# Two transformer blocks on one core: rope operands of 128 rows, evictions ahead of a panel's last split, the latents' inverse root moved from the transposes to the eviction

## What is computed

```python
# first block
h = rms_norm(x, norm_g)
qa, ka, va, ga, qb, kb, vb, gb = split(h @ w_in)                  # 2048 x 8192
ya = stick_breaking_attention(qa, ka, va)                         # 8 heads of 128
yb = chunk_band_attention(qb, kb, vb, q_gain, k_gain, rel_bias)   # 8 heads of 128
x = x + concat(ya * silu(ga), yb * silu(gb)) @ w_out
# second block; c gives six rows: mod = silu(c) @ w_ada + b_ada
sh1, sc1, gt1, sh2, sc2, gt2 = split(mod, 6)
z = (rms_norm(x, g_pre_mix) * (1 + sc1) + sh1) @ w_in_2
cq, ckv, kr, qs, ks, vs, gates = split(z)                         # 768, 512, 64, 2048, ...
q = rms_norm(cq, g_q_lat) @ w_uq        # MLA: 16 heads of 128 + 64 (rope)
kv = rms_norm(ckv, g_kv_lat) @ w_ukv
s = (q_nope @ k_nope.T + rope(q_rope) @ rope(kr).T) * 192 ** -0.5 # causal softmax, @ v
mix = (sigmoid(g_a) * o_mla + sigmoid(g_b) * o_window) @ w_o
x = x + gt1 * rms_norm(mix, g_post_mix)
u = causal_conv3((rms_norm(x, g_pre_ffn) * (1 + sc2) + sh2) @ w_up)
x = x + gt2 * rms_norm((silu(u_gate) * u_up) @ w_down, g_post_ffn)
```

## Time and profile before

| | |
|---|---|
| median of 3 runs | 1977.7 us (1974.12 to 1988.61) |
| profiled execution | 1984.85 us |
| its span | 1982.5 us |
| TensorE busy | 1933.0 us, 98% |
| VectorE busy | 1360.7 us, 69% |
| ScalarE busy | 1049.2 us, 53% |
| GpSimd busy | 119.0 us, 6% |
| mean granted clock of TensorE | 0.997 of 2.4 GHz |

### The profile page before, as it was taken

How to read it: one execution, slowest core, us unless ns; L and a number is a source line. 1 busy time by engine, 2 the same in 40 slices (tenths; PEclk the granted TensorE clock), 3 DMA queues, 4 the chain that set the end, 5 groups by cost and what they waited for, 6 DMA issues and landing times.

```text
span 1982.5 us, 30450 instructions
## 1 busy us (share of the span) xinstructions
PE 1933.0 (98%) x9804; PEld 1612.4 (81%) x9804; DVE 1360.7 (69%) x1838; ACT 1049.2 (53%) x1687; POOL 119.0 (6%) x197
## 2 busy tenths in 40 slices
PE   6999999999999999999999999999999999999998
PEld 5888887778888777778888778888888888888886
DVE  5677776667787745558877767777777776655555
ACT  5544545554455554446764444565656655544444
POOL 1000001101000003331110000000000000000000
PEclk9999999999999999999999999999999999999999
DMA  7788776578888853357678875677777765555554
GB/s 255 273 285 266 242 257 222 183 252 291 282 278 288 301 165 115 115 156 216 201 239 282 305 259 168 214 232 231 236 229 228 238 206 185 174 186 190 192 194 143
DMA packets 233657, 444.82 MB, mean 224 GB/s; under 512 B 14189, under 2 KB 105930, under 8 KB 232186
## 3 DMA queue, kind: packets, MB, share of 16 engines
q1 hardware_dynamic: 230890, 430.20, 65.6%
q0 software_dynamic: 2704, 13.82, 2.2%
HBM read 439.72 MB, written 4.24 MB: 224 GB/s over the span
## 4 chain that ended last, share of the span: by engine, by line
PE 86%; DVE 5%; ACT 3%; issue 3%; DMA 2%; SPq 0%; POOL 0%; DVEq 0%; ACTq 0%; POOLq 0%
PE PS L1659 53%; PE PS L1978 17%; PE PS L1979 8%; PE PS L1753 2%; ACT w_hi L621 1%; DVE arena L1075 1%; PE PS L1764 1%; PE PS L1695 1%; PE PS L1756 1%; PE PS L1739 1%; DVE w_lo L1025 1%; DMA ada_raw<-in_w_ada 1%; PE PS L1774 1%; PE PS L1775 1%; PE PS L1772 1%
## 5 line engine op out<-in xcount | busy, mean ns | idle before, releaser
L1025 DVE TENSOR_TENSOR w_lo<-raw,w_hi 128x1024 fp32r<-128x1024 f32 x618 | 755.3, 1224 | 499.4 <-ACT w_hi L621 491.6
L1659 PE MATMUL PS<-w_hi,aT 128*128 128x512 f32 (+1 forms) x3264 | 1046.1, 394 | 10.7 <-DVE arena L1059 2.4
L621 ACT ACTIVATE w_hi<-raw 128x1024 fp32r<-128x1024 f32 x618 | 653.8, 1060 | 643.3 <-PE PS L1659 431.1
L1659 PEld LDWEIGHTS PS<-w_hi,aT 128*128 128x128 f32 x3264 | 612.2, 188 | 152.2 <-issue 10.2
L1659 PE MATMUL PS<-w_lo,aT 128*128 128x512 f32 (+1 forms) x1632 | 633.6, 388 | 0.0
L1978 PE MATMUL PS<-aT,w_hi 128*128 128x512 f32 x1408 | 499.4, 400 | 2.1 <-DVE aT L1154 2.1
L1979 PE MATMUL PS<-aT,w_lo 128*128 128x256 f32 x1408 | 395.9, 281 | 0.0
L1659 PEld LDWEIGHTS PS<-w_lo,aT 128*128 128x128 f32 x1632 | 307.2, 188 | 58.3 <-issue 0.2
L1978 PEld LDWEIGHTS PS<-aT,w_hi 128*128 128x128 f32 x1408 | 265.0, 188 | 68.2 <-DVE aT L1154 2.3
L1979 PEld LDWEIGHTS PS<-aT,w_lo 128*128 128x128 f32 x1408 | 266.5, 189 | 0.2 <-issue 0.2
L1075 DVE SCALAR_TENSOR_TENSOR arena<-ada_raw,silu_c,arena 128x1024 f32<-128x1024 f32 x192 | 247.6, 1289 | 10.6 <-DMA ada_raw<-in_w_ada 10.4
(11 more groups left out here) (215 smaller groups left out, 1298.8 us busy)
## 6 DMA issues: line engine op xcount, KB each, us to landing
raw<-in_w_in SPq DMA_DIRECT2D x256, 512.0 KB, 3.9
ada_raw<-in_w_ada SPq DMA_DIRECT2D x192, 512.0 KB, 4.8
raw<-in_w_up SPq DMA_DIRECT2D x176, 512.0 KB, 3.5
raw<-in_w_down SPq DMA_DIRECT2D x88, 512.0 KB, 3.8
raw<-in_w_out SPq DMA_DIRECT2D x32, 512.0 KB, 5.4
raw<-in_w_o SPq DMA_DIRECT2D x32, 512.0 KB, 5.4
raw<-in_w_uq SPq DMA_DIRECT2D x18, 512.0 KB, 4.9
raw<-in_w_ukv SPq DMA_DIRECT2D x16, 512.0 KB, 4.0
```

The lines of the kernel that those rows point to most:

```text
L621: nc.scalar.activation(w_hi[:, m % RING, :], raw[:, m % RING, :], ACT.Copy).then_inc(hi_ready, 1)
L1025: nc.vector.tensor_tensor(w_lo[:, m % RING, :], raw[:, m % RING, :], w_hi[:, m % RING, :].bitcast(F32), ALU.subtract).then_inc(lo_ready, 1)
L1659: mm = pe.matmul(dst, l, r, start=first and j == 0, stop=last and j == 2)
```

## The change

1. `krT` and `qrT` get 128 rows instead of 64; GpSimd sets rows 64 to 127 to zero once, after the key's rope part is transposed. ScalarE still writes 64 rows.
2. VectorE and ScalarE evict a panel ahead of their split of slot 7 instead of behind it: `copy_out` in the QKV panels, `add_out` in the projection with w_out, `o_out` and `mix_squares` in that with w_o, and ScalarE's evictions of the latent panels (the 320-column one too).
3. In the stick-breaking panels the head pieces (with `sb_P`) stand between the split and the ada piece, not behind both. In the band panels `stage_b` stands at the start of its slot.
4. The latents are transposed without a diagonal. Their inverse root is the scale of ScalarE's evictions of Q and KV; a semaphore `lat_inv` says that it is there. The squares of the 768 columns of cq go to SBUF instead of PSUM, so that the transposes may write those banks.
5. `mod_sums(SH2)` stands after the fourth split of the KV stage instead of behind the stage.

```diff
-        krT, qrT = pT[0:ROPE, 1, 0:SEQ], s_sb[0:ROPE, 1, 0:SEQ]
+        krT, qrT = pT[:, 1, 0:SEQ], s_sb[:, 1, 0:SEQ]
...
             pool.wait_ge(kr_T, 1)
+            for rope_T in (krT, qrT):
+                nc.gpsimd.memset(rope_T[ROPE:P, :], 0.0).then_inc(pool_step, 1)
+            pool.wait_ge(pool_step, T.ready(pool_step, 2))
...
-                dst = full[:, 0:width] if width <= PANEL else \
+                dst = s_sb[:, :, :].rearrange("p a b -> p (a b)")[:, 0:width] if width <= Q_RANK else \
...
             for slot in range(SLOTS):
+                if slot == SLOTS - 1:
+                    copy_out(lambda s: LATR[:, s, PANEL:2 * PANEL])
                 split()
-            copy_out(lambda s: LATR[:, s, PANEL:2 * PANEL])
-            for slot in range(SLOTS):
+            for slot in range(SLOTS - 1):
                 split()
             for s in range(ST):
                 products(s)
...
                     .then_inc(acc_free[s], 1)
+            split()
...
+            act.wait_ge(lat_inv, 1)
...
-                                             PS[:, 2 * half + s, :], ACT.Copy).then_inc(acc_free[s], 1)
+                                             PS[:, 2 * half + s, :], ACT.Copy,
+                                             scale=stat[:, 10 + s:11 + s]).then_inc(acc_free[s], 1)
...
             with T.loop(3, **GATED, ready_act_step=2) as i:
                 for slot in range(SLOTS):
-                    split()
-                mix_squares(i + 1)
+                    if slot == SLOTS - 1:
+                        mix_squares(i + 1)
+                    split()
...
             def qkv_b(p):
                 for slot in range(SLOTS):
+                    if slot == SLOTS - 1:
+                        copy_out(lambda s: QKV_B[:, s, ds(p * PANEL, PANEL)])
                     g1_slot(slot, p)
-                copy_out(lambda s: QKV_B[:, s, ds(p * PANEL, PANEL)])
...
                 for slot in range(SLOTS):
+                    if slot + 1 in START_B:
+                        stage_b(i * 2 + START_B.index(slot + 1))
                     g1_slot(slot, i + 6)
...
-                    if slot + 1 in START_B:
-                        stage_b(i * 2 + START_B.index(slot + 1))
...
                 for slot in range(SLOTS):
-                    g1_slot(slot, p + 12)
+                    split()
                     heads(slot, start, before)
+                    g1(slot, p + 12)
...
                     inverse_rms(2, 2 * ST)
-                    diagonals(2, 2 * ST)
+                    nc.vector.nop().then_inc(lat_inv, 1)
...
-            with T.loop(4, ready_hi_ready=4) as i:
+            for _ in range(4):
+                split()
+            mod_sums(SH2, B_UP1)
+            with T.loop(3, ready_hi_ready=4) as i:
...
-                if slot == 2:
-                    pe.wait_ge(rows_ready, T.ready(rows_ready, 2))
...
-                    transpose_group(slot - 2, lambda s, k: LATR[:, s, P * k:P * (k + 1)], lambda k: 0 if k < QT else ST)
+                    transpose_group(slot - 2, lambda s, k: LATR[:, s, P * k:P * (k + 1)])
```

More of the change, by code:

```diff
@@ L260, in block_kernel @@
         kr_staged, kr_T, kr_ready = sem("kr_staged"), sem("kr_T"), sem("kr_ready")
+        lat_inv = sem("lat_inv")
         acc_zeroed, row_landed, ffn_row_landed = sem("acc_zeroed"), sem("row_landed"), sem("ffn_row_landed")
@@ L605, in _ @@
             nc.gpsimd.dma_start(ADA_GT2[0:1, :], b_ada_2[:, GT2 * D:(GT2 + 1) * D]).then_inc(ffn_row_landed, 16)
-            pool.wait_ge(rows_ready, 12)
+            pool.wait_ge(rows_ready, 10)
             nc.gpsimd.dma_start(G_FFN, bass.AP(g_post_ffn_2.tensor, 0, [[0, P], [1, D]])).then_inc(ffn_row_landed, 16)
@@ L670, in after_T @@
                     if kind == "mla":
-                        nc.scalar.activation(qrT, PS[0:ROPE, B_S1, 0:SEQ], ACT.Copy)
+                        nc.scalar.activation(qrT[0:ROPE, :], PS[0:ROPE, B_S1, 0:SEQ], ACT.Copy)
                     w = SEQ if kind == "swa" and j else 2 * SEQ
@@ L742, in products, with copy_out @@
                     act.wait_ge(chunk_used, T.ready(chunk_used, chunks))
-            def copy_out(dst, chunks=SLOTS):
+            def copy_out(dst, chunks=SLOTS, row_scale=None):
                 for s in range(ST):
@@ L748, in copy_out @@
                     d = dst(s)
-                    nc.scalar.activation(d, PS[:, s, 0:d.shape[-1]], ACT.Copy).then_inc(acc_free[s], 1)
+                    nc.scalar.activation(d, PS[:, s, 0:d.shape[-1]], ACT.Copy,
+                                         scale=row_scale(s) if row_scale else 1.0).then_inc(acc_free[s], 1)
             def gate(func, gates=GATES[1]):
@@ L889, in _ @@
                     split()
-                    copy_out(lambda s: KV[:, s, ds(i * 1024 + PANEL * j, PANEL)], VT // 2)
+                    copy_out(lambda s: KV[:, s, ds(i * 1024 + PANEL * j, PANEL)], VT // 2,
+                             lambda s: stat[:, 12 + s:13 + s])
             nc.scalar.preload_act_table_set("natural_log_exp_and_others")
@@ L1323, in _ @@
                 for slot in range(SLOTS):
+                    if slot == SLOTS - 1:
+                        copy_out(lambda s: QKV_A[:, s, ds(i * PANEL + 2048, PANEL)])
                     g1_slot(slot, i + 10)
-                copy_out(lambda s: QKV_A[:, s, ds(i * PANEL + 2048, PANEL)])
             def out_of(kind, i, j):
@@ L1366, in _ @@
             for slot in range(SLOTS):
+                if slot == SLOTS - 1:
+                    add_out(PANEL)
                 split()
                 ada_piece(ADA_SC2, 1, slot, 0)
-            add_out(PANEL)
             mod_sums(SC1, B_T)
@@ L1372, in _ @@
                 for slot in range(SLOTS):
+                    if slot == SLOTS - 1:
+                        add_out((i + 2) * PANEL)
                     split()
                     ada_piece(ADA_SC2, i + 2, slot, 0)
-                add_out((i + 2) * PANEL)
             gain(0, C_PREMIX, SC1)
@@ L1416, in _ @@
             HEADS4 = dict(ready_scores_done=4, free_p_transposed=4, ready_s_read=4, ready_p_done=4, ready_o_ready=4)
-            mod_sums(SH2, B_UP1)
             def panel(p, start, before, out, acc=None):
@@ L1501, in _ @@
                 for slot in range(SLOTS):
+                    if slot == SLOTS - 1:
+                        o_out(i + 1)
                     split()
                     ada_piece(ADA_SH2[1], i + 1, slot, 8)
-                o_out(i + 1)
             mean(0, [D], 4)
```

2 lines of the change are left out of this document (1 added, 1 removed).

## The result

The changed kernel took 1949.6 us (median of 4 executions, 1945.4 to 1951.1) beside 1976.3 us (4, 1974.1 to 1988.6) of the kernel before on the same chip: ratio 0.9839, 95% interval 0.9814 to 0.9863. On another chip it took 1949.5 us beside 1979.3, ratio 0.9851 (0.9823 to 0.9878). Forecast were 1949.0, with 1941 to 1963 as the range.

The account below looks back on a forecast made before the run. The prediction took TensorE's row of matmuls, busy 98% of the span, as the bound. Its terms, 12.3 + 5.5 + 4.0 + 1.8 + 2.9 + 4.0 - 1.6 = 28.9 us, gave 1949 us from 1977.7, range 1941 to 1963.

Parts of the forecast that it names:

- A: MLA head scores: rope operands padded to 128 rows remove four row-count changes per head, gaining 12.3 us (bounds 0 to 12.3).
- first rival: MLA scores: padding gains nothing, the cost belonging to accumulating fp32 pairs; 16.6 us left, 1961.2 us; chance 12%.
- B: Stick-breaking panels: masked product ahead of the ada piece removes nearly all TensorE waits for it, 5.5 us (bounds 4.5 to 6.2).
- C: Panel ends: VectorE evicting before the last split removes TensorE's waits for copies, 4.0 us (bounds 2.4 to 4.4).
- D: Band panels: staging the band heads first in the slot removes four TensorE waits, 1.8 us (bounds 1.2 to 1.9).
- E: Latents: inverse root at eviction removes the diagonal wait and 20 passes, less slower ScalarE copies; 2.9 us (bounds 1.5 to 4.0).
- F: SH2 sums moved into the KV stage: removes a 2.4 us pause and 1.6 us of slow clock, 4.0 us (bounds 2.3 to 4.3).
- second rival: Half of everything but A is given back at waits that others set: 20.6 us gain, 1957.2 us; chance 13%.
- G: End of the second block's last output panel: splits behind the evictions delay the mean and its chain, a loss of 1.6 us.
- third rival: Late splits starve the weight ring at panel ends, costing 43 us: 14 us slower in all, 1992 us; chance 3%.
- likeliest case: Whole kernel: the terms hold as summed, its own range about 1942 to 1956 us; chance 72%.

Follow-up runs that it names:

- e1: Changed kernel with the rope operands back at 64 rows, everything else kept: 1962.8 us, ratio to before 0.9914.
- e8: Changed kernel with 64-row rope operands, each MLA head's q·k passes first, then its rope passes (scores not the reference's): 1955.6 us.
- e7: Changed kernel with VectorE's evictions in the QKV panels and the w_out projection behind the last split again: 1955.5 us, ratio to before 0.9893.
- e4: The kernel before, run once more unedited: 1978.6 us, ratio 1.000.
- e9: Changed kernel with the third latent panel's weight chunks loaded 320 columns wide instead of 512: 1948.9 us, ratio to before 0.9866.
- e12: The changed kernel once more, unedited, on another chip: 1949.5 us, ratio to before 0.9851.
- e11: Changed kernel with the edits of e9, e10 and e2 together: 1952.2 us, ratio to before 0.9861.
- e6: Changed kernel with the sums for SH2 behind the KV stage again: 1955.7 us, ratio to before 0.9873.
- e10: Changed kernel with w_ukv chunks issued ahead of the same step's modulation weights in the KV stage: 1947.8 us, ratio to before 0.9855.
- e3: Changed kernel with latents transposed by diagonals and evicted with a constant scale again, earlier evictions kept: 1954.1 us, ratio to before 0.9879.
- e2: Changed kernel with the second block's output projection evictions and squares behind the last split again: 1948.5 us, ratio to before 0.9848.

## Why the prediction was right

The time and the range held, and the outcome is the one given the largest chance: faster by more than the 1% that the prediction draws as its line (the interval ends at 0.9863). Term by term, forecast against measured:

- **A, 12.3: 12.3 at the scores, 10.8 to 11.9 in the time.** The one on which a rival stood. Less its wait for GpSimd's staging, the MLA stage takes 12.3 us less than in either execution of the kernel before; that wait, 1.2 and 0.2 before, is 1.5 now and gives the difference back. e1 takes back 11.9 us, and e8 about half of it by order alone, so the cost belongs to the change of row count and not to the accumulating pair. The first rival is refuted. The rule of the Trainium skill (TensorE: Matmul & The Clock Gate, section "LDWEIGHTS (loading the stationary operand)"), that a load of few rows takes as long as one of 128, agrees with e8's loads, 0.52 us beside 0.53. The passes themselves are no cheaper with 64 rows either: four take 0.85 us and four with 128 rows 0.75, each with one change behind it. What doesn't follow from the rule is that padding is worthless: it removes the changes. The passes after the change start 0.11 and 0.22 us apart, as foreseen.
- **B, 5.5: 4.7 to 4.8.** Right in kind. Left are two waits, 0.71 and 0.87 us, where I expected one of about 0.4 in all.
- **C, 4.0: 4.8** without W_OUT, where 3.5 of the 4.0 were forecast. The step that was off is the price of a wait: 0.16 us on top of the listed time, where e7 shows 0.27. The seven waits of e7 are also longer, 2.8 us where the list before has 2.4; e4 has 3.1. The output projection of the second block gains nothing from it, as foreseen: its waits are 2.3 us in 3 before and after.
- **D, 1.8: 2.2**, by difference.
- **E, 2.9: about 0.7 net, and known to 2 us only.** The two stages together gain 5.4 us; F's 4.2 and about 0.5 for C at a panel end of W_OUT leave 0.7. By single executions the 5.4 is 3.4 to 7.3. The waits and passes went as computed (diagonals gone, 20 passes, 0.45 us a chunk). What failed is that all else would keep up. VectorE's low half of the latents, which TensorE never waited for, now ends 1.5 us late (0.6 to 2.6 in the variants without diagonals), as the rows under e9 show: about half of the time saved at the transposes (1.0 + 2.2 us) is waited for there. The 0.5 us for the eviction of the 320-column panel did not come: that wait is 0.8 us (1.1 in e12) where it was 0.6 (0.9 in e4), and the split ahead of the eviction waits 1.6 us for w_in. The price of the scale from a column did come: TensorE waits 0.31 us at the first two panel ends of the Q stage, where the first profile has no wait. The third, 2.2 us there (1.2 in e12), was 0.9 (1.9 in e4). This is the second rival's mechanism, at this one place; all together, B to F gave 17.0 of the 18.2 forecast (the first five rows of the table).
- **F, 4.0: 4.2.** Both parts as computed, the pause and the slow chunk behind it; the clock is 1.00 where MLA begins.
- **G, -1.6: -1.7.** VectorE's chain is later by 1.69 us, as worked out. The sign that I gave for it, a wait of 2.8 us before the transposes, came in e7 alone (2.96): elsewhere the dummy transposes run into that time at the lower clock, so the wait shown is 0 or 1.3. I had named a clock drop only as something that follows a longer pause; here it comes without one, and lies beside the late chain instead of adding to it. With the old order the same 1.7 us stay lost when the drop is long (e11).

The third rival, a starved ring, did not come anywhere: no wait of TensorE names VectorE's split among its releasers in either execution of the changed kernel. The touched stages sum to 26.7 us where 28.9 were forecast, with A, B and E above what the stages gained and C, D and F below; that the medians came within 1 us of the forecast is partly luck: the kernel before has a spread of 15 us, and the base of the forecast, 1977.7, is 1.4 above the median beside which the change was measured. One slip of the sum did not matter: the upper bounds of the terms add up to 31.5 us, so the likeliest case's own range ends at 1946, and the 1942 given for it does not follow from them. One small wait in the output projection of the first block, which the sum doesn't have, comes from VectorE being earlier: its eviction adds x, which is reloaded, and that had not landed (0.70 us of TensorE at 450.23; the row is VectorE's; e6, e10 and e11 have this wait too, e12 and the others do not):

```profile
449.40 1.29 DVE L1374 TENSOR_TENSOR arena<-arena,PS 128x512 f32<-128x512 f32 x2 [1.92 <-DMA arena<-in_x]
```

Open: why the low clock at the end of W_O comes in both profiles of the changed kernel and in nine of its ten variants (not in e7) and in neither of the kernel before, and how much of the unsteady 1 to 3 us of the latents belongs to the loads of w_in, how much to those of w_ada.

## What to carry to other kernels

Where short matmuls alternate between operands of different row counts, pad or regroup them: look for a weight load that is idle on "issue" and starts with its matmul. A wait removed in a stage that the loads feed can come back as a wait for the next engine in line, here VectorE, held by a load of its own and then without slack; read the waits and the idle time of the engines that consume the loads before counting it. And undoing one edit of a set measures it only if the others don't move what it waits for (e3, e11); compare stages, not times, when the effects are a few us.

## What the runs showed of the hardware that I had not expected

A change between 64 and 128 rows costs about 0.2 us, twice the spacing of a 128-column pass.

A wait of TensorE ahead of a weight matmul costs 0.27 us more than the list shows: 0.16 because the matmul before it is shown longer than its spacing, and 0.11 because the matmul behind it is followed 0.31 to 0.34 instead of 0.23 us later (seven places in e7).

The last stage (up and down projection), which no edit touches and in which TensorE's list has one wait of 0.6 us in either kernel, has two speeds from one execution to the next, both at a granted clock of 1.00. Stretches of 100 us in it, before and then after:

```profile
1300.00:1400.00 100.00, 100.00 (x568) 86.76 (x567) 76.33 (x106) 61.02 (x87) 0.00 (x0) 1.00 0.71 230
```

```profile
1300.00:1400.00 100.00, 100.00 (x579) 87.39 (x578) 78.78 (x113) 61.63 (x86) 0.00 (x0) 1.00 0.72 236
```

568 or 579 matmuls in the same time; the 512-column ones are 236 or 230 to 232 ns apart. The slower speed was in the profiles of before, e1, e2 and e3, the faster in the others, e4 among them. It is 9 us of the span, more than any term but A, and fits the spread of the kernel before (1974 to 1989): the four profiled executions at the slower speed took 7 to 11 us more than the medians of their kernels. What sets it, no run here shows.

The granted clock can fall to 0.50, the 1.2 GHz level, while TensorE is busy without a gap: it did so among 32 one-column matmuls and 60 identity transposes in eleven of twelve profiles of the changed kernel and its variants, and in neither of the kernel before.
